# Finishing each expert's tokens inside the experts' loop instead of behind it

## What is computed

```python
h  = x + W_out [ PoolMix(u) ; RMSNorm(GLA(q, k, v, alpha)) * silu(r) ]   # from RMSNorm(x) @ W_in
hn = RMSNorm(h)
g  = argmax softmax(hn @ W_rg)                      # one of 4 groups
e1, e2 = top-2 of softmax(hn @ W_re) in that group  # of 8 experts, 32 in all
gates = p_group * top_v / sum(top_v)
ffn_e(x) = (silu(x @ W_eg[e]) * (x @ W_eu[e])) @ W_ed[e]       # 1024 -> 512 -> 1024
y  = RMSNorm(h + gates[0]*ffn_e1(hn) + gates[1]*ffn_e2(hn)) * norm_final
```

## Time and profile before

| | before |
|---|---|
| median of 3 runs | 1104.29 us (1102.71 to 1104.57) |
| the profiled execution | 1103.76 us, of which the span of the trace is 1101.9 us |
| TensorE busy (PE) | 1012.4 us, 92% of the span |
| VectorE (DVE) | 417.4 us, 38% |
| ScalarE (ACT) | 240.8 us, 22% |
| GpSimd (POOL) | 104.8 us, 10% |
| moved by DMA | 262.17 MB, 238 GB/s in the mean |

### The profile page before, as it was taken

How to read it: one execution, slowest core, us unless ns; L and a number is a source line. 1 busy time by engine, 2 the same in 40 slices (tenths; PEclk the granted TensorE clock), 3 DMA queues, 4 the chain that set the end, 5 groups by cost and what they waited for, 6 DMA issues and landing times.

```text
span 1101.9 us, 32850 instructions
## 1 busy us (share of the span) xinstructions
PE 1012.4 (92%) x14634; PEld 822.7 (75%) x14634; DVE 417.4 (38%) x909; ACT 240.8 (22%) x506; POOL 104.8 (10%) x172
## 2 busy tenths in 40 slices
PE   5999999999999999875999999999999999999920
PEld 5786777768685958435888898898888888988910
DVE  1434443535253535243432332332322323323338
ACT  2352232323332321210111111011111111111123
POOL 0110101010110101001111011011110110110000
PEclk9999999999999999986999999999999999999965
DMA  8900000000000000384999999999999999999557
GB/s 272 402 5 39 1 39 0 38 0 38 4 34 38 0 38 1 152 322 173 373 375 393 405 399 411 408 404 401 398 410 403 395 409 404 397 405 401 215 214 300
DMA packets 50850, 262.17 MB, mean 238 GB/s; under 512 B 8205, under 2 KB 10701, under 8 KB 42618
## 3 DMA queue, kind: packets, MB, share of 16 engines
q1 hardware_dynamic: 41050, 234.05, 53.8%
q0 software_dynamic: 7168, 18.10, 4.8%
q10 hardware_dynamic: 2592, 9.44, 2.1%
HBM read 241.84 MB, written 26.80 MB: 244 GB/s over the span
## 4 chain that ended last, share of the span: by engine, by line
PE 91%; DVE 5%; DMA 2%; issue 1%; ACT 1%; SPq 0%; ACTq 0%; DVEq 0%; POOLq 0%; POOL 0%
PE bank L1412 31%; PE bank L1178 18%; PE bank L1303 11%; PE bank L1423 10%; PE bank L1230 6%; PE bank L1429 5%; PE bank L1166 4%; DVE arena L1144 1%; DVE arena L1142 1%; PE bank L1279 1%; DMA arena<-in_w_in 1%; DVE arena L1150 1%; PE bank L1237 1%; PE bank L1296 1%; PE bank L1290 1%
## 5 line engine op out<-in xcount | busy, mean ns | idle before, releaser
L1178 PE MATMUL bank<-xnT,arena 128*128 128x128 f32 x1728 | 201.5, 278 | 4.9 <-DMA arena<-in_w_in 3.5
L1178 PEld LDWEIGHTS bank<-xnT,arena 128*128 128x128 f32 x1728 | 197.1, 193 | 7.6 <-DMA arena<-in_w_in 4.0
L1412 PEld LDWEIGHTS bank<-xnT,arena 128*64 128x64 f32 x4096 | 171.8, 138 | 8.9 <-issue 8.9
L1412 PE MATMUL bank<-xnT,arena 128*64 128x96 f32 x4096 | 175.0, 248 | 2.2 <-issue 2.2
L1412 PEld LDWEIGHTS bank<-hnT,arena 128*64 128x64 f32 x4096 | 169.6, 137 | 7.4 <-issue 7.4
L1412 PE MATMUL bank<-hnT,arena 128*64 128x96 f32 x4096 | 172.8, 246 | 0.6 <-issue 0.6
L1026 DVE TENSOR_SCALAR mixT<-mixT 128x384 f32<-128x384 f32 x32 | 11.5, 360 | 324.0 <-ACT mixT L692 324.0
L1303 PE MATMUL bank<-arena,mixT 128*128 128x512 f32 x288 | 127.8, 602 | 3.0 <-DVE mixT L859 3.0
L1303 PEld LDWEIGHTS bank<-arena,mixT 128*128 128x128 f32 x288 | 54.9, 193 | 69.4 <-issue 65.7
L1423 PE MATMUL bank<-arena,silu_r 128*32 128x384 f32 x768 | 86.0, 487 | 0.5 <-issue 0.5
L1429 PE MATMUL bank<-arena,silu_r 128*32 128x256 f32 x384 | 85.9, 380 | 0.0
(11 more groups left out here) (193 smaller groups left out, 934.8 us busy)
## 6 DMA issues: line engine op xcount, KB each, us to landing
arena<-in_w_eg SPq DMA_DIRECT2D x32, 2048.0 KB
arena<-in_w_eu SPq DMA_DIRECT2D x32, 2048.0 KB
arena<-in_w_ed SPq DMA_DIRECT2D x32, 2048.0 KB, 15.4
hn_rows<-hs ACTq DMA_DIRECT2D x18, 512.0 KB, 3.5
arena<-pick_rows SPq DMA_DIRECT2D x16, 512.0 KB, 10.1
arena<-in_w_in SPq DMA_DIRECT2D x3, 2048.0 KB, 14.5
arena<-in_w_out SPq DMA_DIRECT2D x1, 4096.0 KB, 25.7
out_y_prompt<-arena SPq DMA_DIRECT2D x8, 512.0 KB, 3.5
```

Of the source, the lines that this page charges most:

```text
L1178: last = mm(out, w_in_sb[:, k, a:b], xnT[:, k, :], start=k == 0, stop=k == KD - 1)
L1412: last = mm(out[q * SW:(q + 1) * SW, n * BLOCK:(n + 1) * BLOCK], w[:, k, m * P + q * SW:m * P + (q + 1) * SW], rowsT[b][:, k, :], start=k ...
```

## The change

The finish of a token moves into the experts' loop. Of the two experts of a token, the one with the lower number only keeps its row in `y_dram`; the other one finishes the token.

- For every slot three more numbers are carried through the ranking: the slot's own gate, the gate of the token's other pick, and the rms of h; a fourth is the other expert's number. So `M_tok` (32 columns for each pick) becomes `M_val` (five times 32), `mark` multiplies 160 columns, and `slot_of` holds the sums. `back_weights` now comes ahead of `back_rank`. In the last tile `mark` is split in two, so that `idx_i` comes from the first part. `places()` then makes four lists of row numbers for each expert, out of bounds where the slot has nothing to do: where to keep, where the other row lies, and where in `y_prompt` and in `y_sample` to put.
- `y_dram` is filled with zeros by one DMA during the first tile, and `norm_final` is loaded ahead of the experts.
- POOL issues for each expert: `fetch_other` (copies of the lists and weights, then an indirect DMA of the other rows out of `y_dram` into `other[b]`, behind the previous expert's `keep`), the gather of expert e + 2, `keep` (an indirect DMA of `ye` to `y_dram`), and `put` (two indirect DMAs of `done` to `y_prompt` and `y_sample`).
- ScalarE makes `h_slots` = hn of the slot times the rms, a copy of 96 by 1024 with a change of order of the columns, ahead of its copies into `ye`; behind them it takes square, logarithm and exponential.
- VectorE has `finish` behind the next expert's turned rows: other row times its gate plus h, plus own row times its gate, then the norm into `done[b]`. These buffers lie in `h_all`.
- The loads, sums, norms and stores of the end go; for n_x > 0 a version of them stays under the `If`.

The core of the diff (left out are buffers, the lines that make the lists, the removed lines of the old scatter and of the end on ScalarE and VectorE, and the overflow path):

```diff
+        h_slots = h_all[0:BLOCK, 0, :]
+        other = [h_all[0:BLOCK, 1 + b, :] for b in range(2)]
+        done = [h_all[0:BLOCK, 3 + b, :] for b in range(2)]
+        g_fin = h_all[:, 5, :]
...
+            sp.wait_ge(s["setup_pool"], 4)
+            flat_hs = hs[:, :, :].rearrange("p k n -> p (k n)")
+            sp.dma_start(y_dram.rearrange("(r p) n -> p r n", p=P), flat_hs.unsqueeze(1).to_broadcast([P, PICK_ROWS // P, D])).then_inc(s["zeros_stored"], 16)
...
+            sp.wait_ge(s["hs_ready"], TILES)
+            sp.dma_start(g_fin, norm_final.partition_broadcast(P)).then_inc(s["g_fin_in"], 16)
...
             for b in range(2):
+                sp.wait_ge(prompt_out[b], 16 * (NE // 2))
+                sp.wait_ge(sample_out[b], 16 * (NE // 2))
                 sp.wait_ge(ye_stored[b], 16 * (NE // 2))
-            for i in range(TILES):
-                for k, y in ((0, y1[i]), (1, y2[i])):
-                    at_row = (k * TILES + i) * P
-                    sp.dma_start(y[0:OUT_ROWS[i], :], y_dram[at_row:at_row + OUT_ROWS[i], :]).then_inc(y_in[i], 16)
-            for i in range(TILES):
-                sp.wait_ge(out_ready[i], 1)
-                if i == 0:
-                    sp.dma_start(y_sample, y2[i][0:SAMPLE, :]).then_inc(s["outs_stored"], 16)
-                else:
-                    sp.dma_start(y_prompt[(i - 1) * P:i * P, :], y2[i]).then_inc(s["outs_stored"], 16)
-            sp.wait_ge(s["outs_stored"], 16 * (2 * PAIRS + 2 + TILES))
+            sp.wait_ge(s["outs_stored"], 16 * (2 * PAIRS + 2))
...
+            pool.wait_ge(s["zeros_stored"], 16)
...
+            def keep(t, b):
                 e = 2 * t + b
...
+                wait_parted(pool, s["ye_ready"], YE_STEPS * (e + 1), s["parted"])
+                nc.gpsimd.indirect_dma_start(y_dram, bass.IndirectOffsetOnAxis(ap=now_at[b][:, KEEP_AT:KEEP_AT + 1], axis=0), ye[b], None,
+                                             bounds_check=PICK_ROWS - 1, oob_is_err=False).then_inc(ye_stored[b], 16)
+            def put(t, b):
+                e = 2 * t + b
+                wait_parted(pool, s["done_ready"], e + 1, s["parted"])
+                nc.gpsimd.indirect_dma_start(y_prompt, bass.IndirectOffsetOnAxis(ap=now_at[b][:, PROMPT_AT:PROMPT_AT + 1], axis=0), done[b], None,
+                                             bounds_check=SEQ - 1, oob_is_err=False).then_inc(prompt_out[b], 16)
+                nc.gpsimd.indirect_dma_start(y_sample, bass.IndirectOffsetOnAxis(ap=now_at[b][:, SAMPLE_AT:SAMPLE_AT + 1], axis=0), done[b], None,
+                                             bounds_check=SAMPLE - 1, oob_is_err=False).then_inc(sample_out[b], 16)
+            def fetch_other(t, b):
+                e = 2 * t + b
+                if not (isinstance(t, int) and t == 0):
+                    wait_parted(pool, prompt_out[b], 16 * t, s["parted"])
+                    wait_parted(pool, sample_out[b], 16 * t, s["parted"])
                     wait_parted(pool, ye_stored[b], 16 * t, s["parted"])
...
+                nc.gpsimd.tensor_copy(now_at[b][:, :], idx_t[:, bass.ds(e, 1), :].rearrange("p a n -> p (a n)")).then_inc(s["now_ready"], 1)
+                nc.gpsimd.tensor_copy(now_w[b][:, :].unsqueeze(2), slot_of[:, OWN_W:RMS + 1, bass.ds(e, 1)]).then_inc(s["now_ready"], 1)
+                wait_parted(pool, s["now_ready"], 2 * e + 2, s["parted"])
+                if not (isinstance(t, int) and e == 0):
+                    wait_parted(pool, ye_stored[1 - b], 16 * (t + b), s["parted"])
+                nc.gpsimd.indirect_dma_start(other[b], None, y_dram, bass.IndirectOffsetOnAxis(ap=now_at[b][:, OTHER_AT:OTHER_AT + 1], axis=0),
+                                             bounds_check=PICK_ROWS - 1, oob_is_err=False).then_inc(other_in[b], 16)
+            def fetch_rows(t, b):
+                wait_parted(pool, s["pe_eT"], 2 * t + b - 1, s["parted"])
+                wait_parted(pool, s["h_slots_ready"], 2 * t + b - 1, s["parted"])
+                gather(t, b)
             gather(0, 0)
             gather(0, 1)
...
+            pool.wait_ge(s["idx_t_ready"], 1)
+            fetch_other(0, 0)
+            fetch_rows(1, 0)
+            keep(0, 0)
+            put(0, 0)
...
+            with pool.Fori(1, NE // 2 - 1) as t:
                 for b in range(2):
...
+                    fetch_other(t, b)
+                    fetch_rows(t + 1, b)
+                    keep(t, b)
+                    put(t, b)
+            t = NE // 2 - 1
+            fetch_other(t, 0)
+            keep(t, 0)
+            put(t, 0)
+            fetch_other(t, 1)
+            put(t, 1)
+            keep(t, 1)
...
+                if first:
+                    act.wait_ge(s["zeros_stored"], 16)
...
+            final.per = 2
             def expert(t, b, first=False):
                 e = 2 * t + b
                 act.wait_ge(s["pe_g"], e + 1)
                 if not (first and b == 0):
                     act.wait_ge(s["hid_ready"], 2 * e)
                 A(sig[:, 0:NH], bank[2 + b][:, 0:NH], ACT.Exp, scale=-1.0).then_inc(s["sig_ready"], 1)
+                act.wait_ge(s["now_ready"], 2 * e + 2)
+                act.wait_ge(rows_in[b], 16 * t + 16)
+                if not (first and b == 0):
+                    act.wait_ge(s["other_added"], e)
+                A(natural(h_slots), turned(rows[b]), ACT.Copy, scale=now_w[b][:, 2:3]).then_inc(s["h_slots_ready"], 1)
                 act.wait_ge(s["pe_d"], e + 1)
                 if not first:
                     act.wait_ge(ye_stored[b], 16 * t)
...
                     A(ye[b][:, half * OWN:(half + 1) * OWN], bank[6 + half][0:BLOCK, 0:OWN], ACT.Copy).then_inc(s["ye_ready"], 1)
                 for g, (n, c) in enumerate(REST_AT):
                     A(ye[b][g * TG:(g + 1) * TG, 2 * OWN:D], bank[n][BLOCK:P, c:c + REST], ACT.Copy).then_inc(s["ye_ready"], 1)
+                final.begin(e)
+                act.wait_ge(s["fin_ready"], e + 1)
+                if not first:
+                    act.wait_ge(prompt_out[b], 16 * t)
+                    act.wait_ge(sample_out[b], 16 * t)
+                final.then(A(done[b], other[b], ACT.Square, scale=D ** -0.5, accum_out=slot_rstd[b][:, :]))
+                final.then(A(slot_rstd[b][:, :], slot_rstd[b][:, :], ACT.Ln, bias=eps[0:BLOCK, 0:1]))
+                A(slot_rstd[b][:, :], slot_rstd[b][:, :], ACT.Exp, scale=-0.5).then_inc(s["frstd_ready"], 1)
...
+            def back_weights(j, first=False):
...
+                rank(V.tensor_copy(vals[:, OWN_W, 0:1], rt[:, 5:6]))
+                rank(V.tensor_tensor(vals[:, OWN_W, 1:2], rt[:, 5:6], rt[:, 9:10], ALU.mult))
+                rank(V.tensor_tensor(vals[:, OTHER_W, 0:1], rt[:, 5:6], rt[:, 9:10], ALU.mult))
+                rank(V.tensor_copy(vals[:, OTHER_W, 1:2], rt[:, 5:6]))
+                rank.then(V.tensor_copy(vals[:, RMS, :], rms_all[:, bass.ds(j, 1)].to_broadcast([P, PICKS])))
+                rank(V.tensor_copy(gate_all[:, bass.ds(j, 1), :].rearrange("p a k -> p (a k)"), vals[:, OWN_W, :]))
+            def spread(a, b):
+                Mk = M[:, :, :, :].rearrange("p k g e -> p k (g e)")
+                return V.tensor_tensor(M_val[:, :, a:b, :], Mk.unsqueeze(2).to_broadcast([P, PICKS, b - a, NE]),
+                                       vals[:, a:b, :].rearrange("p v k -> p k v").unsqueeze(3).to_broadcast([P, PICKS, b - a, NE]), ALU.mult)
+            def back_rank(j, first=False, last=None):
...
+                if last:
+                    spread(ROW, ROW + 1).then_inc(s["onehot_ready"], 1)
+                    last()
...
+                    spread(OWN_W, VALS).then_inc(s["onehot_ready"], 1)
...
             def back_idx(j):
                 dve.wait_ge(s["pe_idx"], j + 1)
...
+                V.tensor_tensor(flat, flat, bank[7][0:BLOCK, 192:192 + VALS * NE], ALU.add).then_inc(s["idx_added"], 1)
...
+            dve.wait_ge(s["pe_idx"], TILES + 1)
+            dve.wait_ge(s["idx_ready"], 1)
...
+            def places():
+                st = once.then
...
+                st(V.tensor_tensor(early, other_e, con("iota_e", BLOCK), ALU.is_lt))
...
+                V.scalar_tensor_tensor(out=idx_t[:, :, PROMPT_AT], in0=tok, scalar=float(-P), in1=late, op0=ALU.add, op1=ALU.add).then_inc(s["idx_t_ready"], 1)
...
                 moe.end()
                 if not last:
                     rows_turned(e + 1, 1 - b)
+                finish(t, b)
+            def finish(t, b):
+                e = 2 * t + b
+                dve.wait_ge(other_in[b], 16 * t + 16)
+                dve.wait_ge(s["h_slots_ready"], e + 1)
+                V.scalar_tensor_tensor(out=other[b], in0=other[b], scalar=now_w[b][:, 1:2], in1=h_slots,
+                                       op0=ALU.mult, op1=ALU.add).then_inc(s["other_added"], 1)
+                dve.wait_ge(s["other_added"], e + 1)
+                dve.wait_ge(s["ye_ready"], YE_STEPS * (e + 1))
```

(51 more changed lines are left out.)

177 lines of the change are left out of this document (104 added, 73 removed).

## The result

The changed kernel takes 1144.64 us (median of 4 runs, 1141.34 to 1150.72) against 1103.5 (4 runs on the same chip, 1102.62 to 1104.57): 1.0379 times, 95% interval 1.033 to 1.0428. That is slower, as forecast, inside the range, and 18 us above the forecast time. The profiled execution took 1142.5, its span 1140.7.

What follows compares the result with a forecast made beforehand. TensorE bounds the kernel before; after the change, 28 rounds of 18.6 us from expert 2's finish at 581.0 reach 1101.8, the last expert 1118.2, the end 1124.7, plus 1.9 around the span: 1127 us, range 1086 to 1177.

Steps and rivals of the forecast that it cites:

- The gain at the end: Behind the last matmul: all 49.0 us go; one expert's own finish, 13.2 us, stays.
- The front: Ahead of the experts: larger mark product 1.3 us, places() and the second half of the marks 0.5, together +1.8 us.
- the zeros: Fill of y_dram ahead of the experts: 9.44 MB, 23 us on idle DMA engines, costing nothing; uncovered, some 12 us.
- The start: First experts: slots(), 7.6 us of VectorE, falls behind expert 1's finish; expert 2's down product ends at 574.3.
- The round: Each expert: row landed to done 5.7, to next fetch's issue 4.2, landing 8.7; 18.6 us against TensorE's 16.84.
- closed round: Experts' loop: finish, puts, next fetch and its landing wait on each other in turn, setting 28 rounds of 18.6 us.
- two puts in a row: POOL, between done and the next fetch: 0.94 us each; a gap would make that step 5.1 for 4.2; none taken.
- The landing: Other rows' fetch, issue to landing, in each expert: 8.7 us taken, bounds 4.0 and 10.5.
- Rival "the fetch is hidden": Experts' loop: fetch lands after 4.0 us, round 13.9, TensorE stays the bound; 1076 to 1086 us; chance 0.1.
- Its remark on full DMA engines: Experts' stage: 34.5 more rows an expert, 0.35 us, add up to 10 us over 29 experts if weight buffers lack slack.
- Rival "the clock falls": TensorE's waits ahead of each down product lower its clock; product loses about 2.8 us, round 19.2, time 1144; chance 0.09.

Runs made afterwards that it cites:

- e1_late: Changed kernel, whole computation, each expert's finish one expert later, slots() behind the first finish, two h_slots buffers: 1130.97 us, 1.0257.
- e4_no_fetch: Changed kernel without the indirect DMA that fetches the other rows, and without its wait: 1111.69 us.
- b1_pair: Kernel before the change, plus a second scatter of ye right behind each expert's first, to a tensor nobody reads: 1131.21 us.
- e2_one_put: Changed kernel without the put to y_sample, which is not written: 1150.06 us.
- after_less: Changed kernel with half of each down weight not loaded from the third expert on: 1141.73 us.
- f1_spaced: Changed kernel, finish one expert later, each indirect DMA with its own list copy just ahead, order put, keep, put, gather, fetch: 1107.95 us, 1.0045.
- e3_small_h_slots: Changed kernel with ScalarE's copy into h_slots cut to 8 columns: 1144.74 us.
- f1_less: Like f1_spaced, but only half of each down weight is loaded from expert 3 on: 1076.91 us.
- b2_apart: Kernel before the change, plus a second scatter of ye 2.0 us behind each first, with a copy and a wait between: 1131.52 us.
- b3_whole: Kernel before the change with down weights loaded as 16 KB runs a partition, gate and up products taking every fourth column: 1255.41 us, 1.1372.

## Why the prediction came out as it did

- *The gain at the end*: 13.2 predicted behind the last matmul, 14.4 measured. Right.
- *The front*: +1.8 predicted, +1.9 measured; the zeros land 46.3 us after their issue, hidden as said.
- *The start*: 574.3 predicted for expert 2's down product, 577.93 measured. The mechanism, slots() behind expert 1's finish, holds (e1_late removes it); hid came at 570.7 for 569.0, and the product, behind a wait of 10.42 us and begun at the lower clock (0.73 in the window 570 to 578), took 7.0 for 5.3, which the sum did not hold.
- *The round*: 18.6 predicted, 18.91 measured in the mean. That the number is near is luck, for the reason given holds only in part, and this is the step that failed: "So there is a closed round from one normalisation to the next" was taken to set every round. In the changed kernel it sets three. In the others TensorE's own pauses, behind two puts 1.2 us apart, give 0.9 of the 1.41 above 16.84 (17.74 in e4_no_fetch, without any fetch); the other 0.5 is hid's second half, which keeps 1.3 to 1.4 us behind the fetch's issue while the landing varies. If the issue is what holds it, that closes a round of another kind, without the landing: issue to hid 1.4, to the down product 0.6, product 5.4, to done 6.5, to the next issue 4.4, together 18.3; that it does is not shown. At that pace the fetch lands in 3.3 to 8 us, too early to hold TensorE up. The prediction weighed two puts in a row as a matter of POOL's time and never as a cost to TensorE; b1_pair shows that cost with nothing else changed. The closed round is real: remove the pauses (e2_one_put) or lighten the DMAs (after_less) and it binds, at 19.0 and 19.1.
- *The landing*: 8.7 was taken. Measured 3.3 to 15.2 in the changed kernel; where the round through it binds, 9.7 (e2_one_put) and 8.9 (after_less) in the mean of experts 3 to 29. So its size was near, and its effect on most rounds was not. By the Trainium skill ("DMA: Bandwidth & Descriptors", section "Anatomy of one DMA — SWDGE (gpsimd) path") the estimate was 2.9; the lowest landings come near it, and the late ones are five times that.
- *Rival "the fetch is hidden"*: in most rounds it is, and the kernel is slower all the same. Its remark on full DMA engines, 0.35 us an expert by bytes, was the third limit, under-sized: f1_spaced loses 1.5 us a round to it from expert 13 on.
- *Rival "the clock falls"*: in the changed kernel only behind the four waits of over 5 us; the 0.41 us waits ahead of hid leave it at 1.00, as the window 700 to 800 shows. That shorter waits can be enough is seen in e2_one_put: behind two waits of 2.0 us the granted clock fell to its lower level (1.2 GHz) for 3.4 us, and the down product took 7.07 us for 5.39, a loss of 1.7 where the rival had 2.8. It is not always so: a wait of 3.1 us in e3_small_h_slots left the clock at 1.00.

Three limits lie close together above TensorE's 16.84: its pauses with the late hid (18.25), the closed round (19.0 to 19.1 where it binds), the transfers of the weights (18.4 to 18.7). None of the three is a fixed length: the closed round is shorter where the fetch lands early, and b1_pair's transfers fit into 17.7. Lifting one lets the next through, which is why e2_one_put and after_less gain nothing. The 34.6 us at the end would be gained only with all three lifted; f1_less, which lifts them by leaving out loads, gains 26.8. The best whole version, f1_spaced, lifts two and is 0.45% slower than the kernel before; none that beats it was found.

Open stays why close indirect DMAs stop TensorE, what holds VectorE behind the fetch's issue, why one fetch lands in 3.5 us and another in 14, and why the weights' transfers slow down. Neither bytes nor number of the indirect DMAs is enough for the last: in 850 to 950 us b1_pair has 2.50 us a MB and b2_apart, with the same DMAs, 2.58.

## What to carry to other kernels

Work moved from a tail into a loop in which TensorE and the DMA engines are full already is paid once for each turn: 1.4 us a turn over 29 turns, 40.9 us, undid a gain of 34.6. Cost each new indirect DMA three times: in its queue's order, in what it does to the DMA engines, and by how closely it follows the one ahead of it. When a round is near several limits, a prediction of its length can be right for the wrong limit; the row to look at is who waits for whom, not the length.

## What the hardware showed that was not expected

- Two indirect DMAs issued 1.2 us apart by GpSimd cut a running series of matmuls, by about 0.9 us in two pieces, some 0.8 us behind the second (b1_pair); at 2.0 us, with a copy and a wait between them, nothing is cut (b2_apart).
- With four or five indirect DMAs an expert the weights' transfers take 2.56 (e2_one_put) to 2.76 us a MB (after_less) between 850 and 950 us, for 2.49 with two (before) and 2.50 and 2.58 with three (b1_pair, b2_apart).
- Behind a wait of 2.0 us ahead of a product the granted clock fell, twice in e2_one_put, from 1.00 to 0.5 for 3.4 us; behind one of 3.1 us in e3_small_h_slots it did not.
- A stationary operand taken at every fourth column loads in 217 ns for 138, and its matmul takes 284 for 248 (b3_whole).
